# Rotary embeddings in a two-block mixer kernel: partners' rows exchanged by DMA instead of rotation products

## What is computed

```python
def apply_rope(t, cos, sin):
    t1, t2 = jnp.split(tf, 2, axis=-1)
    out = jnp.concatenate([t1 * cos - t2 * sin, t2 * cos + t1 * sin], axis=-1)

def rotary(x, pos):
    x1, x2 = x[..., :half], x[..., half:]
    return jnp.concatenate([x1 * cos - x2 * sin, x1 * sin + x2 * cos], axis=-1)
```

## Time and profile before

| | |
|---|---|
| median of three executions | 2366.75 us (2366.61 to 2367.82) |
| profiled execution | 2367.09 us |
| its span, first to last instruction | 2365.3 us |
| mean granted clock of TensorE | 0.999 |
| TensorE busy | 2348.6 us, 99% |
| VectorE busy | 1570.5 us, 66% |
| ScalarE busy | 1201.0 us, 51% |
| GpSimd busy | 116.5 us, 5% |
| DMA engines | 16 engines busy 53% of the span, 172 GB/s |

### The profile page before, as it was taken

The page is one execution under the profiler, slowest core; times in us unless marked ns, Lnnn a source line. Parts: engine busy times, 40 slices in busy tenths (PEclk is TensorE's granted clock), DMA queues, the critical chain, the costliest instruction groups (busy, mean ns, idle before and its releaser), DMA issues.

```text
span 2365.3 us, 52326 instructions
## 1 busy us (share of the span) xinstructions
PE 2348.6 (99%) x23022; PEld 2300.9 (97%) x23022; DVE 1570.5 (66%) x1416; ACT 1201.0 (51%) x1214; POOL 116.5 (5%) x74
## 2 busy tenths in 40 slices
PE   9999999999999999999999999999999999999998
PEld 8999999999999999999999999999999999999998
DVE  6766777865675568777556656866656656866655
ACT  5545655544454456565445444736445444735443
POOL 0000251000000003500000000000000000000000
PEclk9999999999999999999999999999999999999999
DMA  8656454555555554445655565513655664513653
GB/s 287 204 194 184 131 163 134 188 193 192 184 196 195 195 174 143 144 143 173 207 192 176 196 195 165 183 39 126 208 188 179 207 195 164 184 39 126 202 190 106
DMA packets 322781, 406.92 MB, mean 172 GB/s; under 512 B 6480, under 2 KB 291152, under 8 KB 322384
## 3 DMA queue, kind: packets, MB, share of 16 engines
q1 hardware_dynamic: 321488, 400.58, 52.3%
q10 hardware_dynamic: 1152, 4.22, 0.5%
HBM read 403.72 MB, written 1.05 MB: 171 GB/s over the span
## 4 chain that ended last, share of the span: by engine, by line
PE 92%; ACT 3%; DVE 3%; issue 1%; DMA 0%; SPq 0%; DVEq 0%; ACTq 0%
PE ps L339 83%; PE ps L344 8%; ACT w_hi L298 1%; DVE w_lo L303 1%; PE ps L1487 0%; DMA raw<-in_w_ffn_in 0%; DVE pad L1992 0%; DVE x_hl L392 0%; PE ps L2203 0%; ACT coef L1873 0%; ACT x_hl L366 0%; DVE x L2191 0%; DVE rms L2019 0%; ACT k_t L1132 0%; ACT kk L1842 0%
## 5 line engine op out<-in xcount | busy, mean ns | idle before, releaser
L339 PE MATMUL ps<-x_hl,w_hi 128*128 128x256 f32 x7808 | 1344.0, 277 | 2.4 <-issue 0.9
L303 DVE TENSOR_TENSOR w_lo<-raw,w_hi 128x2048 fp32r<-128x2048 f32 x383 | 881.3, 2302 | 466.5 <-ACT w_hi L298 465.8
L339 PEld LDWEIGHTS ps<-x_hl,w_hi 128*128 128x128 f32 x7808 | 1177.4, 188 | 7.0 <-issue 3.2
L339 PE MATMUL ps<-x_hl,w_lo 128*128 128x256 f32 x3904 | 1078.8, 276 | 0.0
L298 ACT CAST w_hi<-raw 128x2048 fp32r<-128x2048 f32 x383 | 731.1, 1911 | 602.6 <-PE ps L339 591.1
L339 PEld LDWEIGHTS ps<-x_hl,w_lo 128*128 128x128 f32 x3904 | 732.9, 188 | 0.0
L339 PE MATMUL ps<-h_hi,w_lo 128*128 128x256 f32 x1408 | 390.3, 277 | 0.0
L339 PE MATMUL ps<-h_hi,w_hi 128*128 128x256 f32 x1408 | 390.3, 277 | 0.0
L339 PE MATMUL ps<-h_lo,w_hi 128*128 128x256 f32 x1408 | 390.2, 277 | 0.0
L339 PEld LDWEIGHTS ps<-h_hi,w_lo 128*128 128x128 f32 x1408 | 265.2, 188 | 0.0
L339 PEld LDWEIGHTS ps<-h_hi,w_hi 128*128 128x128 f32 x1408 | 265.2, 188 | 0.0
(11 more groups left out here) (455 smaller groups left out, 2471.0 us busy)
## 6 DMA issues: line engine op xcount, KB each, us to landing
raw<-in_w_ffn_in SPq DMA_DIRECT2D x87, 1024.0 KB, 5.1
raw<-in_w_in SPq DMA_DIRECT2D x74, 1024.0 KB, 5.4
raw<-in_w_ffn_out SPq DMA_DIRECT2D x44, 1024.0 KB, 4.9
raw<-in_ffn_w_gate SPq DMA_DIRECT2D x44, 1024.0 KB, 5.3
raw<-in_ffn_w_up SPq DMA_DIRECT2D x44, 1024.0 KB, 5.3
raw<-in_ffn_w_down SPq DMA_DIRECT2D x44, 1024.0 KB, 4.9
raw<-in_w_out SPq DMA_DIRECT2D x16, 1024.0 KB, 5.2
raw<-in_w_mem_kv SPq DMA_DIRECT2D x8, 1024.0 KB, 5.0
```

Of the source, the lines that this page charges most:

```text
L303: nc.vector.tensor_tensor(w_lo[:, slot, :], raw[:, slot, :], w_hi[:, slot, :].bitcast(F32), ALU.subtract).then_inc(lo_ready, 1)
L339: mm = nc.tensor.matmul(out_ap, l, r, start=first and n == 0, stop=last and n == 2, skip_group_check=True)
```

## The change

In both blocks the rotation products of the queries (and of retention's keys) go. ScalarE issues DMAs that copy the partners' rows within SBUF: in the first mixer two for each half of the heads, of 16 partitions by 1024 float32 each (64 KB), as soon as that half's `q_t` is written; in the second mixer four, of 32 partitions by 1024 float32 each (128 KB), once `rqk` is written and after the copy of `z_up`. VectorE waits for the DMAs' semaphore and multiplies the copied rows by the sines in SBUF. The minus signs go into the sine tables: for retention into the constant, for MLA by a per-partition scale of the sine activation. The constant `rot_ret` goes; `rot_mla` stays for the key, without its sign. In the first mixer TensorE waits for the copies of `q_t` where it waited for the rotation. In the second mixer VectorE's split 12 moves from before `bonus` to the place of split 13, and split 13 to behind the fourth level.

```diff
     for m in range(16):
-        rot[64 + 16 + m, 64 + m] = -1.0
+        rot[64 + 16 + m, 64 + m] = 1.0
         rot[64 + m, 64 + 16 + m] = 1.0
     add("rot_mla", rot)
-    rot = np.zeros((P, P))
-    for h in (0, 64):
-        for m in range(32):
-            rot[h + 32 + m, h + m] = -1.0
-            rot[h + m, h + 32 + m] = 1.0
-    add("rot_ret", rot)
+    add("rope_sign", np.where(i % ROPE < ROPE // 2, -1.0, 1.0))
...
-    add("ret_sin", np.sin(ang.astype(np.float64)))
+    add("ret_sin", np.sin(ang.astype(np.float64)) * np.where(i % RET_K < half, -1.0, 1.0)[:, None])
...
-            nc.scalar.activation(rope_sin[:, :], rope_sin[:, :], ACT.Sin)
+            nc.scalar.activation(rope_sin[:, :], rope_sin[:, :], ACT.Sin, scale=C("rope_sign"))
...
                     A(nc.scalar.copy(q_t[0:QK, o:o + 2, :], pair((2, 0)[h] + b)[0:QK]), ("q_t", h, b))
+                need(act, scalar=("q_t", h, 1))
+                half_ = ROPE // 2
+                for a in range(2):
+                    d0, s0 = NOPE + a * half_, NOPE + (1 - a) * half_
+                    act.dma_start(rot_tmp[d0:d0 + half_, 4 * h:4 * h + 4, :],
+                                  q_t[s0:s0 + half_, 4 * h:4 * h + 4, :]).then_inc(q_swapped, 16)
                 split(20 + h)
...
-            need(dve, tensor="q_rot")
-            V(TTo(rot_tmp[r, :, :], bank4(0)[r], sin8, ALU.mult), "rot", True)
-            V(TTo(q_t[r, :, :], q_t[r, :, :], cos8, ALU.mult))
+            dve.wait_ge(q_swapped, l * 64 + 64)
+            V(TTo(rot_tmp[r, :, :], rot_tmp[r, :, :], sin8, ALU.mult))
+            V(TTo(q_t[r, :, :], q_t[r, :, :], cos8, ALU.mult), "q_cos", True)
             V(TTo(q_t[r, :, :], q_t[r, :, :], rot_tmp[r, :, :], ALU.add), "q_rope", True)
...
             level(2)
-            need(pe, scalar=("q_t", 1, 1))
-            for b in range(4):
-                last = mm(ps[:, b, :], C("rot_mla")[0:QK, :], q_t[0:QK, 2 * b:2 * b + 2, :])
-            tensor_sig(last, "q_rot")
             need(pe, vector=("gate", "m", 3))
             branch("m", U_OM, 0, om_hi, om_lo, 4)
             level(3)
-            need(pe, vector="rot")
+            need(pe, scalar=("q_t", 1, 1))
             branch("m", U_OM, 1, om_hi, om_lo, 0)
...
             A(nc.scalar.copy(z_up[:, :, :, :], mask16("ident64")), "z_up")
+            need(act, vector="rqk")
+            for d0 in range(0, P, RET_K // 2):
+                s0 = d0 ^ (RET_K // 2)
+                act.dma_start(rqk_tmp[d0:d0 + RET_K // 2, :, :], rqk[s0:s0 + RET_K // 2, :, :]).then_inc(rqk_swapped, 16)
...
             times(rate, e_ng[:, :, :], "b_hat")
-            split(12)
...
             V(TTo(bonus[:, :, :], bank2(2), v_t[:, :, :], ALU.mult), "bonus")
-            need(dve, tensor="rqk_rot")
-            V(TTo(rqk_tmp[:, :, :], bank2(0), sin4, ALU.mult))
-            times(rqk, cos4)
+            dve.wait_ge(rqk_swapped, l * 64 + 64)
+            V(TTo(rqk_tmp[:, :, :], rqk_tmp[:, :, :], sin4, ALU.mult))
+            times(rqk, cos4, "rqk_cos")
...
                     masked(s_ak, "strict_up64", "ak")
-                    split(13)
+                    split(12)
...
                     times(o_ret, o_ret_sq[:, :, :], "o_ret_normed")
+                    split(13)
...
-                if h == 0:
-                    need(pe, vector="rqk")
-                    for b in range(2):
-                        last = mm(ps[:, b, :], C("rot_ret"), rqk[:, 2 * b:2 * b + 2, :])
-                    tensor_sig(last, "rqk_rot")
```

More of the change, by code:

```diff
@@ L911, in program @@
         stat = sb("stat", [P, 32])
+        q_swapped = sem("q_swapped")
         def mix1_sp(sp, l, n, q):
@@ L1752, in program @@
         a_nat = at("a_nat", 8, [P, TT, 512])
+        rqk_swapped = sem("rqk_swapped")
         def small(name, slot):
```

## The result

The changed kernel takes 2377.47 us (median of six executions, 2374.78 to 2380.7) against 2366.98 us for the kernel before beside it (2366.61 to 2367.82): a ratio of 1.0042 [1.0033, 1.0052], **10.5 us slower**. I had forecast 2367.7 with 2373.0 as the upper end. The profiled execution took 2380.7 us (span 2378.9, mean granted clock 0.996), the longest of the six; before it was 2367.09.

A forecast was written before the change was run, and what follows sets the result against it. It took TensorE as the bound (92% of the span), with VectorE's chain 0.6 us behind in the first mixer. Terms: 2 x (2.2 - 1.72) = +1.0 us, giving 2367.7 us by the median, range 2362.5 to 2373.0.

The forecast's parts named there:

- The direction of the first mixer: Each first mixer was to become 2.2 us longer, although 3.44 us of TensorE products are removed there.
- VectorE's chain and its second merge: First mixer: the second merge ends 2.8 us later, TensorE has 0.6 in hand and idles about 4 before the K projection.
- level 3 late: First mixer: TensorE was to stand still about 1.5 us ahead of level 3, waiting for VectorE's level 2.
- the first subtraction of level 3: First mixer: both GpSimd subtractions of level 3 come after VectorE's split 22, making its chain 1.1 us later.
- GpSimd holds the rotation and the cosine: First mixer: reading SBUF, VectorE's rotation waits 0.7 us and its cosine 1.0 us for GpSimd operations.
- the swap of the first mixer: VectorE's wait for it costs nothing: DMAs issued by 313.0, used at 331.6, against 3.0 to 5.4 us to landing.
- the splits: Second mixer: moving VectorE's splits 12 and 13 costs nothing while its idle time lasts; without it 2.3 us.
- The swap's landing in the second mixer: The swap lands 3.0 us after the last issue, at 1537.0, before VectorE finishes `bonus` at 1537.5, so no wait.
- The other end: Second mixer: with a landing of 5.4 us VectorE waits 1.85 us, and the layer still gains, -0.3 us.
- -1.72: Second mixer, per layer: TensorE keeps the whole gain of its two removed rotation products, 1.72 us.
- The issue on ScalarE: First mixer: two DMA issues cost 0.85 us and the wait 0.15, so the cast of unit 21 starts 1.0 later.
- terms 1 to 3: Second mixer's swap, ScalarE's issue, and lower-clock products in the first mixers, 1.6 and 2.9 us, which the sum left out.

The follow-up runs named there:

- e4: The kernel before with all products kept, but VectorE's rotation reads `q_t` in SBUF instead of the rotated queries in PSUM: 2366.91 us, ratio 0.9998.
- e5: The retention (second mixer) part of the change alone, with the moved splits, first mixers as in the kernel before: 2367.66 us, ratio 1.0001.
- e7: e5 with splits 12 and 13 back where they were in the kernel before: 2368.57 us, ratio 1.0004.
- e3: e1 with all four DMAs of a layer issued behind ScalarE's cast of unit 22: 2376.63 us, ratio 1.0041.
- e2: e1 with products of zeros filling TensorE's idle time ahead of level 3 and of the K projection: 2372.75 us, ratio 1.0024.
- e10: The changed kernel with tiny products of zeros where the rotation products stood, eight per first mixer, four per second: 2375.88 us, ratio 1.0035.
- e8: e3 with the two merges the K projection needs ahead of the rotation, level mask and split 24 behind the later merges: 2370.69 us, ratio 1.0015.
- e9: e8 with eight tiny products of zeros per first mixer where the rotation products stood: 2367.50 us, ratio 0.9999.
- e11: The changed kernel with the late issue of e3, the merges of e8 and the order of e6: 2365.30 us, ratio 0.9991.
- e12: e11 with the tiny products of zeros in both places, as in e10: 2363.93 us, ratio 0.9985.
- after: The changed kernel itself, with both parts of the change, against the kernel before: 2377.47 us, ratio 1.0042.
- e1: The MLA (first mixer) part of the change alone, second mixer as in the kernel before: 2379.72 us, ratio 1.0043.
- e6: e5 with `r_hat` ahead of the swap wait, and TensorE's wait for the turned rows moved to the retention's scores: 2365.88 us, ratio 0.9992.

## Why the prediction was wrong

*Right.* The direction of the first mixer, against the 3.44 us of removed products; that VectorE's chain and its second merge become the bound (TensorE waits 4.1 and 2.6 us for `gates_m`, where 4 us each was said); level 3 late by 2.2 us where 1.5 was said; that the first subtraction of level 3 falls behind split 22; that GpSimd holds the rotation and the cosine, by 0.7 and 1.0 us (measured 2.99 and 3.26 us, and e4 isolates the first); the swap of the first mixer, no wait; the splits, nothing (e5 against e7). No run isolates the sines. The rule of the Trainium skill, SBUF — State Buffer, section "Who interferes with whom", agrees with the rows shown here, e4's above all: an operand moved from PSUM to SBUF, nothing else changed, and 2.29 us became 2.98.

*Wrong, term by term.*

1. **The swap's landing in the second mixer**, the step "landing 3.0 us later (the 128 KB of one swap) is 1537.0". It took 4.7 us, and the four issues 2.70 instead of 4 x 0.46 = 1.84. The other end that I kept, a weight load's 5.4 us, covers VectorE's wait (1.85 us said, 1.67 measured), but still gave -0.3 for the layer: it had TensorE's wait for `rqk`, and not its second one, for the retention's mask `ret_s`, nor what is lost further on. -1.72 became about 0: 3.4 us of the sum. A row of the same KB was no price for this swap, and its size isn't all of it: in e3, where four swaps of 64 KB are issued in a row, these land in 4.0 us, against 2.3 for two in a row.
2. **The issue on ScalarE**, "I take 0.85, near the row, and 0.15 for the wait". It cost 1.5 us within the mixer (the 1.8 of the rows, less the 0.3 that lay ahead), 0.6 for each DMA and the rest around them, where 1.0 was said. It reached VectorE's split 23 as 1.5 us instead of 1.1, so the chain costs 2.7 us (e2, layer 0) instead of 2.2.
4. **TensorE's program.** No step had it. "Removing a product is worth its length" leaves out that the instructions behind it shift. The next packet of instructions came late at other products, and the second mixer of layer 1 took 3.4 us more; e10's profile gives all of that back, its median 1.6 us of the total.

With terms 1 to 3 the sum is 2 x (2.7 + 0) + 1.6 + 2.9 = 9.9, and +3.4 for term 4 makes 13.3 of the profiled execution's 13.6. By the median it is 10.5, and which of the clock's and the program's parts is smaller in the other executions, their profiles would have to tell.

*Open.* Why the clock falls in some executions of e8, e9, e11 and e12 and not in others, and behind one wait of 2.15 us and not behind the other; why the packet of instructions comes late at one place and not at another; and how much of the 3.4 us an average execution pays.

## What to carry to other kernels

Where TensorE is followed by another engine's chain with 0.6 us to spare, a product removed from TensorE is idle time, and idle time may be paid for twice, by the clock. Shorten the other chain first (here: merges ahead of the rotation, DMAs issued off ScalarE's path, nothing behind the swap that needn't be), and only then remove the product. Cost a DMA on an engine's queue by its issue time on that engine as well as by its landing, and measure a landing between partitions of SBUF, with as many issues in a row as the kernel will have, rather than take a load's. When a stage that was not touched changes, compare at which instruction, not at which time, TensorE waits.

## What the runs showed of the hardware that was not expected

- A DMA from SBUF to SBUF of 64 KB over 16 partitions, two in a row, landed in 2.3 us (after), four in a row in 4.0 (e3); one of 128 KB over 32 partitions, four in a row, in 4.7 (after) to 4.9 (e5); a load of 128 KB from HBM had taken 3.0. The eight issues of 128 KB in after took 533, 610 and 855 ns (shortest, median, longest), against 0.46 us for the issue of the earlier trace rows.
- In the first mixers the granted clock fell behind idle stretches of 4.1 us (after and e3) and, in one layer of two, of 1.8 to 2.2 us (after, e1, e10), and stayed at 1.00 when they were filled (e2).
- TensorE has waits of up to 1.6 us (e6) at fixed places of its program, multiples of 127 products apart, which end 1.19 to 1.55 us after a 16 KB packet of its instruction queue has ended (46 of 46 in 14 profiles). One of 1.07 us in the chunk recurrence was followed by a window at 0.68 (e8); the same code with 16 more tiny instructions a layer had neither (e9).
